# The delta rule's triangular inverse in blocks of 32, and the router's norm laid over the output projection

## The reference, cut to what matters

```python
# gated delta rule, per head: a unit lower triangular system
L = jnp.where(strict, jnp.einsum('bhncd,bhnsd->bhncs', kb, kc) * decay, 0.0)
sol = lax.linalg.triangular_solve(L + jnp.eye(CHUNK), rhs, lower=True, unit_diagonal=True)
# end of the mixer, norm ahead of the router
x = x + g1[:, None] * token_mixer(...)            # its last step: o @ w_out
h = rms_norm_2(x, norm2_w) * (1.0 + sc2[:, None]) + sh2[:, None]
scores = sigmoid(h @ w_router)                     # then top-k experts
```

## Time and profile before

| what | us |
|---|---|
| median of 3 runs | 1706.25 (1704.33 to 1706.89) |
| the profiled execution, its own time | 1702.79 |
| its span | 1701.1 |
| PE busy, share of the span | 1504.4, 88% |
| VectorE busy | 997.1, 59% |
| ScalarE busy | 673.6, 40% |
| mean granted clock of TensorE | 0.933 |

### The profile page before, as it was taken

The page is one execution under the profiler, slowest core; times in us unless marked ns, Lnnn a source line. Parts: engine busy times, 40 slices in busy tenths (PEclk is TensorE's granted clock), DMA queues, the critical chain, the costliest instruction groups (busy, mean ns, idle before and its releaser), DMA issues. The chain is left out here.

```text
span 1701.1 us, 29858 instructions
## 1 busy us (share of the span) xinstructions
PE 1504.4 (88%) x12212; PEld 1250.1 (73%) x12212; DVE 997.1 (59%) x1515; ACT 673.6 (40%) x920; POOL 136.7 (8%) x249
## 2 busy tenths in 40 slices
PE   6978697999999989976447889999999999999996
PEld 6976385999999989846337767777777777777773
DVE  5645564576775468733654646666666665656653
ACT  4342333546443445401533324444444444444442
POOL 7000000001000001000100020000000010000000
PEclk9986699999999999969678889999999999999998
DMA  7422300445554746430232558888889889888880
GB/s 253 166 99 75 125 4 2 149 164 183 198 199 152 170 100 150 162 135 0 79 122 81 205 200 337 337 334 334 338 329 331 331 338 336 337 334 334 339 325 25
DMA packets 113224, 349.32 MB, mean 205 GB/s; under 512 B 9633, under 2 KB 33392, under 8 KB 96448
## 3 DMA queue, kind: packets, MB, share of 16 engines
q1 hardware_dynamic: 103184, 315.75, 51.8%
q0 software_dynamic: 8240, 27.40, 5.3%
q10 hardware_dynamic: 1664, 4.26, 0.7%
HBM read 345.15 MB, written 2.23 MB: 204 GB/s over the span
## 5 line engine op out<-in xcount | busy, mean ns | idle before, releaser
L2996 DVE TENSOR_TENSOR weights_lo<-raw_weights,weights_hi 128x2048 fp32r<-128x2048 f32 x99 | 223.8, 2288 | 82.5 <-ACT weights_hi L2900 82.5
L2900 ACT ACTIVATE weights_hi<-raw_weights 128x2048 fp32r<-128x2048 f32 x99 | 185.5, 1910 | 23.5 <-DMA raw_weights<-in_w_gate 19.8
L2702 PE MATMUL bank<-x_hi,weights_hi 128*128 128x256 f32 x544 | 154.8, 285 | 0.0
L2703 PE MATMUL bank<-x_lo,weights_hi 128*128 128x256 f32 x544 | 154.7, 284 | 0.0
L2704 PE MATMUL bank<-x_hi,weights_lo 128*128 128x256 f32 x544 | 154.7, 284 | 0.0
L411 PE MATMUL bank<-in_x_hi,in_w_hi 128*128 128x256 f32 (+2 forms) x456 | 133.3, 292 | 3.7 <-DVE in_w_lo L360 3.7
L411 PE MATMUL bank<-in_x_hi,in_w_lo 128*128 128x256 f32 (+2 forms) x456 | 131.7, 289 | 0.0
L411 PE MATMUL bank<-in_x_lo,in_w_hi 128*128 128x256 f32 (+2 forms) x456 | 131.4, 288 | 0.0
L2782 PE MATMUL bank<-raw_weights,gathered_pair 128*64 128x512 f32 x512 | 113.4, 595 | 0.0
L2702 PEld LDWEIGHTS bank<-x_hi,weights_hi 128*128 128x128 f32 x544 | 105.2, 193 | 2.3 <-issue 1.6
L1534 DVE TENSOR_TENSOR ffn_weights_lo<-weight_ring,ffn_weights_hi 128x2048 fp32r<-128x2048 f32 x33 | 75.6, 2292 | 53.4 <-ACT ffn_weights_hi L1529 53.4
(11 more groups left out here) (607 smaller groups left out, 3737.7 us busy)
## 6 DMA issues: line engine op xcount, KB each, us to landing
raw_weights<-in_w_gate SPq DMA_DIRECT2D x64, 1024.0 KB, 8.9
raw_weights<-in_w_up SPq DMA_DIRECT2D x64, 1024.0 KB, 9.0
raw_weights<-in_w_down SPq DMA_DIRECT2D x64, 1024.0 KB, 7.9
weight_ring<-in_w_in SPq DMA_DIRECT2D x17, 2048.0 KB, 9.2
mixer_memory<-in_w_ada SPq DMA_DIRECT2D x96, 256.0 KB, 3.9
weight_ring<-in_w_ffn_in SPq DMA_DIRECT2D x22, 1024.0 KB, 6.2
weight_ring<-in_w_ffn_out SPq DMA_DIRECT2D x5, 2048.0 KB, 7.7
weight_ring<-in_w_out SPq DMA_DIRECT2D x4, 2048.0 KB, 7.6
```

What stands on the lines that cost most here:

```text
L2702: T.matmul(out_, hi[:, d, cut], x_hi[:, d, :], start=(d == 0), stop=False)
L2703: T.matmul(out_, hi[:, d, cut], x_lo[:, d, :], start=False, stop=False)
L2900: S.activation(w_hi[:, n % 4, :], raw_w[:, k % RAW, :], ACT.Copy).then_inc(s_hi.sem, 1)
L2996: V.tensor_tensor(w_lo[:, n % 4, :], raw_w[:, k % RAW, :], w_hi[:, n % 4, :].bitcast(F32), ALU.subtract).then_inc(s_lo.sem, 1)
```

## The change

The inverse works on the diagonal blocks of 32 side by side. Four blocks of eight matrices are held compactly as `Xc`, `Tc`, `Lc` of 128 partitions by 8x32. Levels 1 to 4 run on them in 8 items of the same order as before; one product group is 16 products of 32x32. After that only the wanted quarters are made: blocks of 64 from two blocks of 32, then the 128 from two of 64.

The folded masks `near` and new ones, `near_lower`, are made in the input projection at tile 23. `kg` and `qg` move to the end of the inverse block. ScalarE copies `L2`, POOL clears `X2`. Pieces of `place` are renamed `place_at`, which changes nothing that runs.

The squares, their sum and the inverse norm go into the output projection as its `between` parts, POOL adding the squares; the four loads go behind the last use of the ring; the scaling and shifting of the norm go to the head of the expert block, and the logits wait for them piece by piece.

```diff
             if m == 23:                                    # input projection, VectorE
+                for i in range(6):
+                    V.tensor_reduce(near[:, i, :], ..., AX.X, ALU.add)
+                for i in range(5):
+                    V.tensor_reduce(near_lower[:, i, :], ..., AX.X, ALU.add)
                 marks["n2"] = dve_s.value                  # setup, VectorE
+                for b in B:
+                    dve_s.on(V.tensor_tensor(Xc[b], X2[b, :, b], wide(near[:, 1, :], b, 2 * GH), ALU.mult))
+                dve_s.on(V.tensor_tensor(Xc, wide(near[:, 0, :], ALL, 2 * GH), Xc, ALU.subtract))
                 dve_s.on(V.tensor_tensor(AT, AT, bc(upper_incl, 2 * GH), ALU.mult))
-                dve_s.on(V.tensor_tensor(kg, mats(k2), eg, ALU.mult))
-                dve_s.on(V.tensor_tensor(qg, mats(q2), eg, ALU.mult))
...
-        triangular_inverse(L2, X2, Tm2, LM2, WW2, P, 4, 2, range(1, 7))
+        todo2 = [(n, g) for n in range(1, 5) for g in range(2)]
+            def _(dve):
+                for i in range(len(todo2) + 2):
+                    if i < len(todo2):
+                        mask(i)
+                    if i >= 2:
+                        update(i - 2)            # Xc and Tc, 128x128 each
+                for b in B:
+                    s_grown.on(V.tensor_copy(X2[b, :, b], Xc[b]))
+                for b in B[0:2]:
+                    s_grown.on(V.tensor_copy(Tm2[b, :, b], Tc[b]))
+                dve.wait_ge(s_far2.sem, s_far2.count(2))
+                s_grown.on(V.tensor_scalar(Tm2[B[1], :, B[0]], strip(bank[1], B32)[B[1]], -1.0, None, ALU.mult))
+                dve_s.on(V.tensor_tensor(kg, mats(k2), eg, ALU.mult))
+                dve_s.on(V.tensor_tensor(qg, mats(q2), eg, ALU.mult))
+            def _(pe):
+                def products(to, left, right, g):
+                    for q in range(4):
+                        for b in B:
+                            mm = T.matmul(to[b, q * B32:q * B32 + B32], left[b, 4 * g + q, :], right[b, 4 * g + q, :], start=True, stop=True)
+                def block_product(i):
+                    pe.wait_ge(s_lm2.sem, i + 1)
+                    if i >= 2:
+                        pe.wait_ge(s_x2.sem, 2 * (i - 1))
+                        pe.wait_ge(s_wc2.sem, i - 1)
+                    s_w2.on(products(bank[g], LMc, Xc, g))
+                def corrections(i):
+                    products(bank[2 + g], Tc, WWc, g)
+                    s_xw2.on(products(bank[4 + g], WWc, Tc, g))
+                # far quarters: 16 products of 32x32, 24 of 32x32, 8 of 64x64, 8 of 64x64,
+                # each group after ScalarE's (and once VectorE's) copy of the one before
...
+        def router_loads(sp):
+            done, by = slot_freed[W_OUT2 + 1]
+            sp.wait_ge(done.sem, by)
+            small_in.on(sp.dma_start(wr, ...), 16)
+            for k in range(3):
+                load_piece(sp, k)
+        def stream_squares(act, m):
+            if m == 0:
+                s_rs3.on(S.activation(rs3[:, 0:1], one_col, ACT.Sqrt))
+            act.wait_ge(dve_s.sem, mixed0 + m + 1)
+            s_sq3.on(S.activation(squares3[:, m, :], xT[:, m, :], ACT.Square))
+            if m == KD - 1:
+                s_rs3.on(S.activation(rs3, bank[0][:, 0:T2], ACT.Sqrt, bias=eps_rms, scale=1.0 / D))
+        def stream_sum(pe, m):
+            if m == KD - 1:
+                pe.wait_ge(s_acc3.sem, s_acc3.count(KD - 2))
+                T.matmul(bank[0][:, 0:T2], ones, squares3[:, 0, :], start=True, stop=False)
+                pe.wait_ge(s_sq3.sem, s_sq3.count(KD))
+                s_sum3.on(T.matmul(bank[0][:, 0:T2], ones, squares3[:, KD - 1, :], start=False, stop=True))
+        # VectorE behind tile 7: V.reciprocal(rs3, rs3); POOL: the tables, then six additions of squares
-        rms_norm(xT, hB, ..., T2, sq2, rs2)
...
-                for c in range(2):
-                    for k in range(KD):
+                for k in range(KD):
+                    pe.wait_ge(s_hbs.sem, s_hbs.count(k + 1))
+                    for c in range(2):
...
+                for j in range(KD):                        # expert block, ScalarE, ahead of split(0)
+                    act.wait_ge(s_hb.sem, s_hb.count(j + 1))
+                    s_hbs.on(S.activation(hB[:, j, :], hB[:, j, :], ACT.Identity, bias=...))
...
+                for j in range(KD):                        # expert block, VectorE, ahead of rest_of(0)
+                    s_hb.on(V.scalar_tensor_tensor(out=hB[:, j, :], in0=xT[:, j, :], scalar=gain2[:, j:j + 1], in1=rs3, ...))
```

More of the change, by code:

```diff
@@ L124, in build, with place_at @@
         first_kept = arena.enter_context(nc.sbuf_tensor("mixer1_kept", [P, FIRST], F32))
-        def place(name, shape, at, dt=F32R):
+        def place_at(name, shape, at, dt=F32R):
             assert at % 8 == 0 and at + int(np.prod(shape[1:])) <= total
@@ L331, in _ @@
                     load_slots(sp, first_slot + n_slots + RING)
+                    if "sp" in between:
+                        between["sp"](sp)
                 @block.scalar
@@ L1177, in _ @@
                     s_wc.on(S.activation(WWs[:, i % 2], four(bank[i % 2]), ACT.Copy))
[L1179 to L1249, removed]
-                        act.wait_ge(s_w.sem, i + 1)
-                        if i >= 2:
-                            act.wait_ge(s_xw.sem, i - 1)
-                        s_wc.on(S.activation(WW[0:width, i % 2], shaped(bank[i % 2]), ACT.Copy))
@@ L1479, in build @@
         arena.close()
-        f_hi = [place(f"ffn_weights_hi{i}", [P, PIECE], i * PIECE) for i in range(CUT)]
-        f_lo = [place(f"ffn_weights_lo{i}", [P, PIECE], (CUT + i) * PIECE) for i in range(CUT)]
+        f_hi = [place_at(f"ffn_weights_hi{i}", [P, PIECE], i * PIECE) for i in range(CUT)]
+        f_lo = [place_at(f"ffn_weights_lo{i}", [P, PIECE], (CUT + i) * PIECE) for i in range(CUT)]
         AT_X = -(-FIRST // 8) * 8
@@ L1598, in build @@
         SECOND = LOW + KD * T2
[L1599 removed]
+        second_kept = place_at("mixer2_kept", [P, SECOND], 0, F32)
         view = Memory(second_kept, 0, SECOND).view
@@ L1994, in build @@
         WW2 = m2b.take(2, 4, P)
+        small_of = lambda ap, at, w: ap.rearrange("p a b c -> p (a b c)")[:, at:at + 2 * GH * w].rearrange("p (m c) -> p m c", c=w)
+        Xc, Tc, Lc, LMc = (small_of(LM2, 256 * i, B32) for i in range(4))
+        WWc, W5, W6 = small_of(WW2, 0, B32), small_of(WW2, 256, B32), small_of(WW2, 512, 64)
+        B = [slice(B32 * j, B32 * j + B32) for j in range(P // B32)]
+        wide = lambda ap, rows, n: ap[rows].unsqueeze(1).broadcast_to([rows.stop - rows.start, n, B32])
+        ALL = slice(0, P)
         lowa = Memory(second_kept, 0, KD * T2 + 12 * (3 + T2))
@@ L2098, in _ @@
             def _(act):
+                for q in range(2):
+                    act.wait_ge(pe_s.sem, marks["turned"] + q)
+                    act.wait_ge(dve_s.sem, marks["lower", q])
+                    act_s.on(S.activation(L2[:, 4 * q:4 * q + 4, :], pair(bank[q]), ACT.Copy))
                 ada_copy(act, ada_w2, 1, bank[7])
-        triangular_inverse(L2, X2, Tm2, LM2, WW2, P, 4, 2, range(1, 7))
+            @block.gpsimd
+            def _(pool):
+                pool_s.on(G.memset(Tm2[0:64, :, 0:64], 0.0))
+                pool.wait_ge(dve_s.sem, marks["cut"])
+                pool.wait_ge(pe_s.sem, marks["turned"] + 1)
+                pool_s.on(G.memset(X2, 0.0))
@@ new lines, in build @@
+        project([o_all], T2, [(W_OUT2 + m // 4, (m % 4) * P, P, 0) for m in range(KD)], mixer_out, W_OUT2, 2,
+                    (place_at("out2_x_hi", [P, KD, T2], AT_PARTS2), place_at("out2_x_lo", [P, KD, T2], AT_PARTS2 + KD * T2),
+                     [place_at(f"out2_w_hi{i}", [P, KD, P], AT_PARTS2 + 2 * KD * T2 + i * D) for i in range(CUT)],
+                     [place_at(f"out2_w_lo{i}", [P, KD, P], AT_PARTS2 + 2 * KD * T2 + (CUT + i) * D) for i in range(CUT)]),
+                    owner=lambda m: "dve",
+                between={"sp": router_loads, "pool": router_tables, "pe": stream_sum, "act": stream_squares, "dve": stream_inverse})
@@ L2925, in _ @@
                 act.wait_ge(s_logits.sem, 1)
-                S.activation(scores, bank[6][:, 0:2 * NE].rearrange("p (a b) -> p a b", b=NE), ACT.Sigmoid).then_inc(s_scores.sem, 1)
+                for c in range(2):
+                    S.activation(scores[:, c, :], bank[6 + c][:, 0:NE], ACT.Sigmoid).then_inc(s_scores.sem, 1)
                 for b in range(4):
```

190 lines of the change are left out of this document (139 added, 51 removed).

## The result

The changed kernel takes 1681.5 us (median of 4 runs, 1678.1 to 1688.5) where the kernel before takes 1706.6 on the same chip (4 runs, 1704.3 to 1707.6): ratio 0.986, interval 0.983 to 0.989. It is faster, by 25 us and not by the 35.5 of the forecast; 1670.7 was 10.8 us too low, and 1681.5 lies half a microsecond above the range. The profiled execution has a span of 1676.4 us, 24.7 less than the 1701.1 of before.

What follows compares the result with a forecast made beforehand. PE bounds most of the kernel, but the inverse is a chain of hand-offs. Inverse 28.0 saved, recurrence 0.9 lost, norm 8.4 saved: 35.5 off 1706.25 gives 1670.7 us, range for 8 in 10 1662 to 1681.

Steps and rivals of the forecast that it cites:

- One item: Inverse loop: 96 records of 32 columns plus two 128x128 updates take 2.04 us (1.80 to 2.28), before 4.34.
- the six periods: Inverse, successive items of the small-product loop after its start: six periods take 12.2 us together.
- the last item: Inverse, end of the small-product loop: its corrections follow the ones before directly, 0.85 us.
- Far quarters: End of the inverse: a pure chain of products, copies and hand-offs making the wanted quarters, 7.4 us.
- The signs of being wrong: Wrong if the period is over 3 us, PE's first recurrence product waits for VectorE, or the expert stage itself changes.
- Start: Start of the inverse: mask, two block products, corrections of item 0, updates and hand-offs, 3.2 us.
- Setup block: Block ahead of the inverse: work removed and added lies beside the weights' arrival, so nought.
- Recurrence: Unchanged code behind the inverse: one more slow group from PE's clock, 0.9 us lost (3.6 lost to 1.8 gained).
- The norm: From tile 7 of the output projection to the expert choice: 8.4 us saved (6 to 9), VectorE's low parts last.
- The masks: Input projection, tile 23: eleven folds instead of six come 1.7 late, costing nought, at worst 1 us.
- The expert stage: Long regular stage behind the choice: equal length, so every microsecond saved ahead of it arrives at the end.

Runs made afterwards that it cites:

- half_products: Changed kernel with the side-by-side products covering only two of the four diagonal blocks, 48 records an item instead of 96; shows time only: 1673.5 us, ratio 0.981.
- doubled: Changed kernel with each small product of the side-by-side loop issued twice, 192 matmul records an item instead of 96: 1701.4 us in one run.
- wide64_four: Changed kernel with the inverse on 64x64 blocks, levels 1 to 5, in four groups of two heads' blocks, four items in flight: 1669.7 us, ratio 0.976.
- four_again: The 64x64 version in four groups (wide64_four) run once more, beside the changed kernel on one chip: 1666.6 us, ratio 0.979.
- norm_only: Changed kernel with the old inverse put back, so only the router's norm stays changed: 1695.5 us against 1705.8 before, ratio 0.9945.
- after_again: The changed kernel itself, unaltered, run again on the same chip and in the same rounds as its rivals: 1682.3 us, ratio 0.986.
- inverse_only: Kernel before with only the new inverse, its setup and its masks; the norm stays behind the projection: ratio 0.9931, 11.3 us less by the medians.
- early_x: Changed kernel with the corrections of X signalled before those of T, the next block product waiting for X alone: 1677.2 us, ratio 0.981.
- wide64_early: 64x64 version in two groups (wide64) with the corrections of X signalled before those of T: 1673.2 us, ratio 0.977.
- filler: Changed kernel with one unused 128x128 by 128x128 product behind each item's corrections, two more matmul records an item: 1684.5 us.
- wide64: Changed kernel with the inverse on 64x64 diagonal blocks, levels 1 to 5 in ten items of 48 records, then one far quarter: 1681.9 us.

## Why the prediction was wrong

- **One item, 2.04 us (1.80 to 2.28): the step that failed**, and by what it left out. 96 records took 1.50 us (1.16 to 1.64 forecast) and an undisturbed period 2.15, in *half_products* 2.12. But the six periods were put at 12.2 and took 16.86, the last item at 0.85 and took 3.42: 7.2 us, which is what *half_products* gave back (6.8). The step priced PE's products by 64 records in a row, 128 instructions, fewer than the 254 between two gaps. A loop of 1536 instructions at 192 an item and 2.04 us asks for 94 a microsecond; 70 come (*doubled*). The nearest sustained loop in reach was the first layer's: 48 records with their loads in 1.40 us, 69 a microsecond. It would have been the warning that nothing had yet been seen at 94; PE is busy all through it, so it shows no limit.
- **A page that names the term.** The Trainium skill, page "Advanced Engine Details and Errata", section "ISA Cache", gives an instruction memory of 32 KB, 128 KB on TensorE, in lines of 16 KB or 256 instructions, "Only 2 cache lines!". The gaps every 254 counted instructions and the 16 KB packets agree with the size of a line; how many lines TensorE has, no run here shows. It gives no rate, so the size of the term had to come from a run.
- **Two rules weighed.** The Trainium skill, page "TensorE: Matmul & The Clock Gate", section "Wait — 56ns, not 53.3ns?", says that the starts of matmuls never come closer than about 25 ns. Here 96 records in 1.50 us are 0.0156 us each, so it does not hold for these products. The Trainium skill, page "TensorEngine Tiling (Array Packing)", section "Gotcha 1: PSUM Pressure", says that different row tiles can't access one PSUM bank at the same time. Here four row positions took 1.50 us for 96 records and two took 1.49 for 48, each group of products into one bank, so that does not hold either.
- **Far quarters, 7.4 (slow bound 8.5): 9.24.** The clock was at its lower level throughout; the two groups of 64x64 took 1.9 and 2.0 us where I took 1.5. In *wide64_four* the second took 1.71, in *four_again*, at clock 1.00, 1.14. The 0.7 above the bound is the first two groups: 32 records on two places took 1.06 and 48 on three about 1.07, where the bound had 0.55 and 0.82, as if spread over four places. The copies and hand-offs came out as priced: 0.06 + 0.87 + 0.97 + 0.68 + 0.62 of the 9.24 us without PE, 3.2. That the clock would be low over all of the inverse was within my bounds but not my middle. Beside the chain it went as said: VectorE's kg and qg are over at 777.84, well before ScalarE's last copy at 780.56.
- **The signs of being wrong.** A period over 3 us did not show it: the six took 2.8 on average, with the block at 32.5 us instead of 21 to 26. And PE's first product of the recurrence does wait for VectorE, but so it did before, so that sign tells nothing.
- **Start, 3.2: 3.02.** Right. **Setup block, nought:** 34.03 us against 34.46 before. Right.
- **Recurrence, 0.9 lost:** 15.80 us against 14.5 before (798.46 to 812.98). Lost 1.3, on the side expected, and it does start at the lower clock. But *norm_only*, with the old inverse in front of it and a granted clock of 1.00 on entry, took 15.84 too (mean clock 0.78, in the changed kernel 0.74, before 0.88). So that the number came out is luck, as far as these profiles tell.
- **The norm, 8.4:** 14.36 us against 22.9, 8.5 saved; by the medians of *norm_only* 10.4. Right in each step, VectorE's low part last, the sixth addition of POOL (900.95) before tile 7 (902.09).
- **The masks, nought, at worst 1: not told apart.** The setup block starts 2.3 us later than before (714.6 against 712.3), but over the twelve profiles with such masks (eleven of the experiments) it starts anywhere from 713.8 to 722.2, and of before there is one profile.
- **The expert stage, equal:** 759.95 us from choice to end against 761.15. Right.

The account of the spans: 8.8 in the inverse, 0.4 in the recurrence, 2.3 ahead of the setup block, 1.6 in branch B behind the recurrence (74.3 us against 72.7), less 0.4, 0.5, 0.1 and 1.2 in setup, projection, norm and experts, is 10.9; missed were 35.5 - 24.7 = 10.8. The 1.6 us of branch B are within what profiles of unchanged code differ by: it took 73.0 in *norm_only*, 72.4 in *after_again* and 71.7 in *four_again*. What stays open: why the clock stays low in the loop of small products even where no gap is left (*half_products*), what starts a packet of instructions, and why *inverse_only* saved 11.3 us where 14 to 16 were expected.

## What to carry to other kernels

Cutting products smaller to use the corners of the array also multiplies the instructions, so count them: this kernel gets 256 in 3.6 to 3.7 us at best, and its loops that asked for more were bound by that. In a profile it shows as idle time without a releaser inside a group, at equal distances in instructions and not in items. A short burst says nothing about it; price a sustained loop by a sustained loop. The block size alone did not decide it here: 64x64 in two groups was no faster than 32x32 (ratio 0.986 both), and either gained once TensorE waited less for VectorE (32x32 0.981 in *early_x*, 64x64 0.977 in *wide64_early* and 0.976 in *wide64_four*, all on one chip and with intervals that overlap).

## What the runs showed of the hardware

- PE's instruction supply: 70 a microsecond sustained at the lower clock (*doubled*, ten refills), 69 in *early_x*. In the changed kernel, *inverse_only*, *doubled* and *early_x* the first gap came only behind 199 records; no run varied the point at which the loop is entered, so how long a loop may be without a gap stays open.
- PE went on 1.24 to 1.57 us after the end of a 16 KB packet of instructions, at each of the 35 gaps of six profiles; the packet itself took 0.9 to 1.4 us, so its transfer is only about a third of the 3.6 us.
- Four 32x32 corners of the diagonal run fully side by side: 96 records over four corners 1.50 us, 48 over two 1.49, at clock 0.50.
- The granted clock: 0.50 over the whole loop of 32x32 products, with gaps and without (*half_products*); 1.00 for 3.4 us of it in *filler*, where PE had been busy nearly without a break for 4 us, and 0.50 again from within the gap of 2.03 us on; 1.00 in the 64x64 loops from 3.3 to 8 us after their start (*four_again* 3.3, *wide64_four* 5.3, *wide64_early* 5.7, *wide64* 8.0).
